# Level products and turns of a triangular inverse on the diagonal quarters of the TensorE array

## The reference

```python
decay = jnp.exp(jnp.where(incl, g[..., :, None] - g[..., None, :], -jnp.inf))
kb = k * beta[..., None]
a_low = jnp.where(strict, jnp.einsum('nhcid,nhcjd->nhcij', kb, k) * decay, 0.0)
tmat = lax.linalg.triangular_solve(eye + a_low, eye, left_side=True, lower=True, unit_diagonal=True)
u = jnp.einsum('nhcij,nhcjv->nhciv', tmat, v * beta[..., None])
# then a scan over chunks: state, v_new = u - w @ state, output, update of the state
```

## Time and profile before

| what | value |
|---|---|
| executions | 3623.45, 3625.92, 3629.67 us (median 3625.92) |
| profiled execution | 3616.41 us, its span 3614.2 us |
| busy: TensorE, its weight loads | 3432.4 us (95%), 2826.6 us (78%) |
| busy: VectorE, ScalarE, GpSimd | 1471.5, 1018.5, 1347.0 us |
| mean granted clock of TensorE | 0.977 |
| level products at levels 0 to 4 (L1435) | 704 instructions, 97.9 us busy |
| turns of the inverse (L1448) | 448 instructions |
| evictions of the turns (L1702) | 112 instructions, 61.7 us busy |

### The profile page before, as it was taken

One profiled execution on the slowest core, in us unless ns is written; L12 is line 12 of the kernel. 1 busy time (PEld: TensorE's weight loads), 2 busy tenths in 40 slices (PEclk: granted clock), 3 DMA queues, 4 the chain that ended last, 5 costly groups with the idle time before them and its releaser, 6 DMA issues. The chain is left out here.

```text
span 3614.2 us, 45557 instructions
## 1 busy us (share of the span) xinstructions
PE 3432.4 (95%) x17928; PEld 2826.6 (78%) x17928; DVE 1471.5 (41%) x2236; ACT 1018.5 (28%) x1737; POOL 1347.0 (37%) x1164
## 2 busy tenths in 40 slices
PE   6999999999999999989999999999899999999998
PEld 5777777767788888878777887888678877777877
DVE  4333333343444444436743333333453134444433
ACT  3334333421334333330131111111212134342221
POOL 4222222224333333333543333443442455554543
PEclk9999999979999999999999999999999999999999
DMA  2010000002111111121311111111231111111122
GB/s 103 30 30 30 30 30 30 30 18 86 49 33 32 38 27 38 27 88 64 129 66 47 46 46 46 46 46 48 81 107 47 53 50 40 49 44 47 58 87 76
DMA packets 104033, 187.72 MB, mean 52 GB/s; under 512 B 32312, under 2 KB 64696, under 8 KB 101184
## 3 DMA queue, kind: packets, MB, share of 16 engines
q1 hardware_dynamic: 103872, 185.48, 16.2%
HBM read 158.33 MB, written 27.12 MB: 51 GB/s over the span
## 5 line engine op out<-in xcount | busy, mean ns | idle before, releaser
L303 PE MATMUL DP<-XH,WH 128*128 128x512 f32 x2608 | 850.1, 407 | 23.3 <-POOL WL L251 23.3
L249 POOL CAST WH<-WRAW 128x1024 fp32r<-128x1024 f32 (+2 forms) x257 | 263.8, 1026 | 1580.3 <-issue 959.8
L303 PE MATMUL DP<-XL,WH 128*128 128x512 f32 x2608 | 811.9, 393 | 0.0
L303 PE MATMUL DP<-XH,WL 128*128 128x512 f32 x2608 | 810.4, 392 | 0.0
L251 POOL TENSOR_TENSOR WL<-WRAW,WH 128x1024 fp32r<-128x1024 f32 (+2 forms) x257 | 588.3, 2289 | 20.7
L303 PEld LDWEIGHTS DP<-XH,WL 128*128 128x128 f32 x2608 | 492.8, 189 | 107.2
L303 PEld LDWEIGHTS DP<-XL,WH 128*128 128x128 f32 x2608 | 493.0, 189 | 106.9
L303 PEld LDWEIGHTS DP<-XH,WH 128*128 128x128 f32 x2608 | 463.2, 190 | 142.2 <-issue 48.1
L848 DVE SCALAR_TENSOR_TENSOR SS<-B,RQ,SBI 128x256 f32<-128x256 f32 (+2 forms) x192 | 74.5, 430 | 312.1 <-PE B L555 312.1
L699 ACT ACTIVATE PP<-SS,NM 128x256 f32<-128x256 f32 (+2 forms) x192 | 88.4, 461 | 257.4 <-DVE NM L855 257.4
L367 DVE TENSOR_TENSOR XR<-XR,B 128x1024 f32<-128x1024 f32 x88 | 106.5, 1219 | 101.6 <-PE B L347 101.6
(11 more groups left out here) (468 smaller groups left out, 5217.8 us busy)
## 6 DMA issues: line engine op xcount, KB each, us to landing
WRAW<-in_w_up SPq DMA_DIRECT2D x44, 512.0 KB, 3.6
WRAW<-in_w_attn SPq DMA_DIRECT2D x36, 512.0 KB, 3.6
WRAW<-in_w_down SPq DMA_DIRECT2D x22, 512.0 KB, 3.6
XR<-in_x SPq DMA_DIRECT2D x8, 1024.0 KB, 8.8
WRAW<-in_w_dn SPq DMA_DIRECT2D x16, 512.0 KB, 3.4
aa_dram<-AA SPq DMA_DIRECT2D x12, 512.0 KB
YY<-yy_dram SPq DMA_DIRECT2D x12, 512.0 KB, 4.1
WRAW<-in_w_lrux SPq DMA_DIRECT2D x10, 512.0 KB, 3.5
```

The costliest lines, as they stand in the source:

```text
L249: pool.tensor_copy(WH[b.slot][:, 0:b.kt, :], WRAW[b.slot][:, 0:b.kt, :]).then_inc(w_hi, 1)
L303: mm = pe.matmul(DP[b.slot][:, half * H:half * H + H], w[b.slot][:, k, :], x[:, k, half * H:half * H + H], start=one, stop=end)
```

## The change

Three steps of the level stage change; nothing else does, and no wait is added or taken away.

- times_a at levels 0 to 4: each matmul with the whole 128x128 array becomes two with a 64x64 quarter of it (rows and columns 0 to 63, then 64 to 127), each with the same 64 moving columns. They write the same columns of PT_U, each its own half of the partitions.
- turn_y: each 128x128 transpose becomes two 64x64 matmuls of a diagonal quarter of YY against the identity. Their results stand in columns 0 to 255 of PT_X instead of 0 to 511.
- take_x copies 256 columns instead of 512, into XC, which lies at the place of XX and holds only the diagonal quarters. times_x reads XC (at level 0 the quarters of XX), in 64x64 matmuls at all levels.

```diff
@@ -1074,6 +1074,7 @@
         AA, YY = ([[x[:, :, e] for e in range(2)] for x in xs] for xs in (AAV, YYV))
         AAV, AA = AAV + AAV[0:1], AA + AA[0:1]
         XX = [at(f"XX{e}", S0 + 34 + 2 * e, [P, 2, 2, P]) for e in range(2)]
+        XC = [at(f"XC{e}", S0 + 34 + 2 * e, [P, 2, 2, 64]) for e in range(2)]
         BL, BY, BT, BW = (at(n, 124 + i, [P, 16, 16]) for i, n in enumerate(("BL", "BY", "BT", "BW")))
         aa_dram = nc.dram_tensor("aa_dram", [8, P + 1, P], F32, kind="Internal").ap()
         yy_dram = nc.dram_tensor("yy_dram", [8, P + 1, P], F32, kind="Internal").ap()
@@ -1432,9 +1433,11 @@
                             mm = pe.matmul(PT_U[e][c, o:o + 64], aa(n)[r, d, h, c], YY[v][e][r, d, h, r],
                                            start=True, stop=True)
                         else:
-                            mm = pe.matmul(PT_U[e][:, o:o + 64].rearrange("p (m b) -> p m b", b=2 << l),
-                                           aa(n)[:, d, h, :], part(YY[v][e][:, d, h, :], l, 1 - d),
-                                           start=True, stop=True)
+                            for g in range(2):
+                                r = half(g)
+                                mm = pe.matmul(PT_U[e][r, o:o + 64].rearrange("p (m b) -> p m b", b=2 << l),
+                                               aa(n)[r, d, h, r], part(YY[v][e][r, d, h, :], l, 1 - d),
+                                               start=True, stop=True)
                 mm.then_inc(lp_ready[e], 1)
 
             def turn_y(n, l):
@@ -1444,8 +1447,10 @@
                     pe.wait_ge(lx_ready[e], turns_done(n, l))
                 for d in range(2):
                     for h in range(2):
-                        o = P * (2 * d + h)
-                        tr = pe.transpose(PT_X[e][:, o:o + P], YY[v][e][:, d, h, :], IDENT)
+                        o = 64 * (2 * d + h)
+                        for g in range(2):
+                            r = half(g)
+                            tr = pe.matmul(PT_X[e][r, o:o + 64], YY[v][e][r, d, h, r], IDENT[r, r], start=True, stop=True)
                 tr.then_inc(lxt_ready[e], 1)
 
             def times_x(n, l):
@@ -1457,9 +1462,10 @@
                 for h in range(2):
                     for d in range(2):
                         o = 256 + 64 * (2 * d + h)
-                        c = half(d) if l == NL - 1 else slice(0, P)
-                        mm = pe.matmul(PT_U[e][c, o:o + 64], XX[e][c, d, h, c], PM[e][c, d, h, :],
-                                       start=True, stop=True)
+                        for g in (d,) if l == NL - 1 else range(2):
+                            c = half(g)
+                            mm = pe.matmul(PT_U[e][c, o:o + 64], XC[e][c, d, h, :] if l else XX[e][c, d, h, c],
+                                           PM[e][c, d, h, :], start=True, stop=True)
                 mm.then_inc(lu_ready[e], 1)
 
             def turn_o(p):
@@ -1699,7 +1705,7 @@
             def take_x(n, l):
                 p, s, e, v = grp(n)
                 act.wait_ge(lxt_ready[e], turns_done(n, l) + 1)
-                act.activation(XX[e][:, :, :, :].rearrange("p d h n -> p (d h n)"), PT_X[e], ACT.Copy).then_inc(
+                act.activation(XC[e][:, :, :, :].rearrange("p d h n -> p (d h n)"), PT_X[e][:, 0:256], ACT.Copy).then_inc(
                     lx_ready[e], 1)
 
             def conv_mid(p, pos):
```

## The result

The changed kernel took 3598.5 us (median of four executions, 3595.1 to 3605.5) against 3627.8 us for the kernel before (four executions), a ratio of 0.993 (95% interval 0.9908 to 0.9953): 17 to 33 us less. The prediction was 3597 us, in a range of 3583 to 3615.

The account below looks back on a forecast made before the run. TensorE was taken to bound stretches one, three and five of each level stage; 1.7 + 2.4 + 3.05 = 7.15 us per pair, 28.6 in four, took 3625.9 to 3597 us, in a range of 3583 to 3615.

Parts of the forecast that it names:

- What bounds it: Level stages: only stretches one, three and five, filled by TensorE, give time; two and four are DRAM round trips of 24 us.
- The waits: TensorE's DMA waits ahead of m = 1 and m = 3 were to grow by some 4 us each.
- stay ahead: Third stretch: the YY read at 1014.90 waits for scan2(1), moves 2 us earlier too, and so does not delay TensorE.
- The sum: All level stages: 1.7 + 2.4 + 3.05 = 7.15 us less per pair, 28.6 us in four pairs.
- The rates: Quarter passes 0.030 us each, 32 in about 1.15 us, turns the same; at half clock 0.060 each.
- Changes of shape: Each switch of array shape between groups costs about 0.1 us, up to four more per level; bounds nothing and 0.33 us.
- First stretch: Levels 0 and 1, to the first aa_dram write: 1.7 us less, with VectorE hiding what times_x saves in level 0.
- Third and fifth stretch: Third stretch 2.4 us less up to the third aa_dram write, fifth 3.05 us less until the next dense product.
- The rival: Clock stays low in stretches three and five after longer DMA waits: 17 us per pair slower, 3694 us; chance 0.08.
- Evictions and turns: Each level: take_x some 0.15 to 0.2 us shorter, turns 0.07 us longer.
- The path is elsewhere: VectorE, ScalarE and DMA chains end the stretches, not TensorE: gain under 7 us, 3620 us; chance 0.12.
- Quarters without overlap: Two quarters writing one bank run one after the other, 0.060 us a pass: 6.5 us per pair slower, 3652 us; chance 0.04.

Follow-up runs that it names:

- e1: The change only at levels 0 and 1 of m = 0 and all levels of m = 1 and 3; level stages 409.6 us, 435.2 before.
- e2: The change only at levels 2 to 5 of m = 0 and at m = 2; level stages 445.2 us against 435.2 before.
- e6: The changed kernel with GpSimd's block inversion stopped after 7 of 14 columns; level stages 365.5 us, 40.8 less than the change.
- e7: The changed kernel with times_a on the whole array again; level stages 446.8 us against 435.2 before, whole-kernel ratio to before 0.9992.
- e8: The kernel before plus 3 and 14 products of constants in the waits ahead of m = 1 and 3; level stages 416.7 us against 435.2.
- e9: The changed kernel plus, ahead of m = 1 and 3, 4 products of constants at once and 13 after block inversion; level stages 402.0 us.
- e11: The changed kernel plus products of constants: 4 and 11 ahead of m = 1, 10 after block inversion ahead of m = 3; level stages 396.5 us.
- e3: The changed kernel with 128x128 transposes and 512-column evictions as before, only the products on quarters; level stages 408.2 us against 435.2 before.
- e4: The changed kernel with all matmuls of one quarter first, then the other's; level stages 428.8 us, 22.5 more than the change.
- e5: The changed kernel plus 10 and 15 products of constants in the DMA waits ahead of m = 1 and 3; level stages 406.9 us.

## Why the prediction was right, and where it was not

*What bounds it.* Right in the main: the three stretches in which TensorE's busy time fills the length gave 25.6 of the 28.9 us (e1), the others none by themselves (e2), and the round trips through DRAM end these (e6). The waits came out otherwise in one place. Ahead of m = 1 the wait grew from 1.9 to 3.7 us to 7.1 to 7.4, as forecast; ahead of m = 3 it was 8.0 us in the mean before and after, and no 4 us were added. The prediction had the YY read of the middle chain "stay ahead". It doesn't: after the change TensorE waits for it, too, for 1.5 to 2.8 us in each pair, ahead of m = 2:

```profile
1030.02 1.15 PE L1438 MATMUL DP<-YY,AA 64*64 64x64 f32 x32 [1.63 <-DMA YY<-yy_dram]
```

That costs nothing by itself, since the third chain ends the fourth stretch anyway.

*The sum.* 28.6 us predicted, 28.9 measured, and that is luck in part: S1 gave 6.5 us (6.8 predicted), S3 and S5 together 24.7 (21.8 predicted), S2 0.8 (none predicted), and S4 took back 3.1 (none predicted).

*The rates.* Right: 0.030 us for a pass in alternating quarters, 1.15 us for 32 of them, the turns 1.10. The rule of the Trainium skill that different row tiles can't access one PSUM bank at a time ("TensorEngine Tiling (Array Packing)", "Restrictions and Gotchas") did not hold here: passes of the two row halves, which write one bank, begin 7 ns apart, and each half goes at the 58 ns per pass that it needs alone. Half clock nearly doubles a pass, to 0.056; 0.060 was taken.

*Changes of shape.* 0.1 us each was taken. No run changes them alone; in the single instructions of the fifth stretch shown above, the first 128x128 product behind the turns begins 0.15 us after the last of them, and the first quarter product of times_x 0.21 us after the last 128x128 one, where the steps inside these groups are at most 0.05 and 0.11 us. That agrees with some 0.1 each.

*First stretch.* 1.7 us predicted, 1.65 measured in pairs 1 to 3 and 1.55 in pair 0. Without times_a nothing is left (e7), and the trace shows what hides the saving of times_x in level 0: the second gram product now waits for the decayed step of VectorE, as the prediction had it.

```profile
976.02 1.13 PE L1394 MATMUL B<-KQ 64*128 64x256 f32 x8 [0.81 <-DVE DQX L1847]
```

*Third and fifth stretch.* 2.4 and 3.05 us predicted, 3.1 and 3.1 measured on the mean of the pairs. That the sum of the two is near is luck, too: one term was too large, and another, the low clock, was not in the sum. At full clock the change is worth 2.1 and 2.1 us (e8, e9, e11), 17 us in four pairs. (In the third stretch TensorE's busy time falls by 3.6 us at full clock, from 23.9 in e8 to 20.3 in e9, and only 2.1 of them count: the stretch ends when ScalarE's evictions of AA are done, in pair 0 of the change at 1030.16, and TensorE waits by then.) With the low clock of before unchanged, as the prediction took it, the prices of before and after (0.475 and 0.44 us for each us) make that some 19 us, where 21.8 were predicted; it is the fifth stretch that was counted too high. The rest, some 6 us, came from low clock that left these stretches: 46.9 us of it lay there before, 33.5 after. The rival took it as longer.

Where it went is seen around the first landing of pair 0, at 993.2 us before and 1006.6 after (columns as in the earlier trace rows; the first two rows are of the kernel before):

```profile
991.30:993.20 1.90, 0.00 (x0) 0.00 (x0) 0.69 (x3) 0.00 (x0) 0.00 (x0) 1.00 1.14 342
993.90:1000.70 6.80, 6.80 (x35) 6.80 (x34) 1.71 (x6) 2.12 (x6) 2.89 (x10) 0.50 0.12 13
...
999.50:1003.10 3.60, 0.02 (x1) 0.00 (x0) 0.75 (x3) 0.00 (x0) 2.81 (x5) 1.00 0.16 18
1003.10:1006.60 3.50, 0.02 (x2) 0.02 (x2) 0.00 (x0) 0.00 (x0) 0.00 (x0) 0.50 0.76 225
1006.60:1009.90 3.30, 3.30 (x62) 3.30 (x64) 0.85 (x2) 0.38 (x1) 0.00 (x0) 0.50 0.40 94
```

Before, TensorE was idle for 1.9 us, and the granted clock was 0.50 for 6.8 us, all of them behind the landing. After, TensorE was idle for 7.1 us, and of the same 6.8 us half passed ahead of the landing, while nothing could run anyway. This is one pair. Over S2 to S5 of all pairs the clock was low for 68 us before and 82 after, so the low clock as a whole grew; but 21 us of it lay in the round trips before and 49 after. And where it lasts longer, the gain goes: in pair 1 it was 3.4 us behind the first landing before and 6.1 after, and the third stretch there is only 1.1 us shorter, against 3.3 to 4.1 in the others. In e2 and e7 more of it lay in S3 and S5 than before. How long it lasts was not forecast and is not explained; that the change gained by it is luck, as far as the prediction goes.

*Evictions and turns.* Wrong in size: 0.2 to 0.35 us per stretch were counted for the evictions, and 0.07 against them for the turns. e3 shows nothing for both together. The rows of level 4 above show why, there: the eviction (L1708) is over at 1063.87, and times_x (L1467) begins at 1064.85, behind scan products that stand between them.

*The rivals.* "The path is elsewhere" is out by e1. Quarters without overlap would have cost 6.5 us per pair; the order that comes nearest to it (e4) gave 1.6 us less than before, since passes still overlapped in part. The low clock in the third and fifth stretch moved the other way. Its price is 0.44 to 0.48 us for each us, so some 15 us more of it per pair would have been needed to eat the 7 us saved, not the 8 that the prediction named.

## What to carry to other kernels

Cut a stage at the points where its DMA chains start and land, and count TensorE's savings only in the pieces that its busy time fills: the same edit gave 25.6 of its 28.9 us there, and nothing by itself in the others. Small products like these belong on alternating quarters of the array, with neighbours in the queue on different ones. Where TensorE waits for a DMA, the price is the wait and then about half of the time that the clock stays low behind it; a few products on constants, timed to end shortly before the data land, gave back most of that here (e11), while products that ended 2.7 us ahead gave nothing (e5) and products that ended after the landing cost their overrun (e9). After a change of TensorE's work, look at the low clock again before the gain is put down to the work.

## What the runs showed of the hardware that was not expected

- A float32 pass with a 64x64 quarter needs 58 ns in its own quarter, whatever the other does; two quarters at once give 0.030 us per pass, quarters in runs of eight instructions 0.042 us (e4).
- A us at a granted clock of 0.50 cost 0.44 to 0.48 us of a stretch in which TensorE is busy for over 90%. A group of products takes 1.95 us at 1.00 and 3.68 at 0.50, quarter passes 0.030 and 0.056, so in a us at 0.50 some 0.53 us of work is done and 0.47 us is lost: nearly all of that reaches the stretch.
- The round trip through DRAM takes 24.0 to 27.6 us for the same work. GpSimd's part of it is 12.1 to 12.3 us in every trip; the rest scatters with the landing of the DMAs, and what delays them is open.
